# Expert steps of 1024 columns with one PSUM bank pair each for gate and up, in place of 512-column steps on two alternating banks

## What is computed

```python
D_MODEL, SEQ, N_EXPERTS, TOP_K, EXPERT_DIM = 1024, 256, 8, 2, 3584

def swiglu(x, w_gate, w_up, w_down):
    return (jax.nn.silu(x @ w_gate) * (x @ w_up)) @ w_down

def moe_swiglu(x, w_router, b_router, w_gate, w_up, w_down):
    xt = x.reshape(-1, D)
    logits = (xt @ w_router).astype(jnp.float32) + b_router.astype(jnp.float32)
    top_val, top_idx = lax.top_k(logits, TOP_K)
    gates = jax.nn.softmax(top_val, axis=-1)
    combine = jnp.sum(jax.nn.one_hot(top_idx, N_EXPERTS) * gates[..., None], axis=1)
    for e in range(N_EXPERTS):
        out = out + combine[:, e:e + 1] * swiglu(xt, w_gate[e], w_up[e], w_down[e])
    return out
# f(x) of every sub-layer goes into x <- LayerNorm(alpha * x + f(x))
```

## Time and profile before

| | us |
|---|---|
| median of 3 runs (1743.3 to 1747.3) | 1747.09 |
| the profiled execution | 1747.38 |
| its span, first to last instruction | 1745.6 |
| gather of the first link to gather of the second | 123.55 |

### The profile page before, as it was taken

How to read it: one execution, slowest core, us unless ns; L and a number is a source line. 1 busy time by engine, 2 the same in 40 slices (tenths; PEclk the granted TensorE clock), 3 DMA queues, 4 the chain that set the end, 5 groups by cost and what they waited for, 6 DMA issues and landing times.

```text
span 1745.6 us, 22452 instructions
## 1 busy us (share of the span) xinstructions
PE 1617.3 (93%) x8768; PEld 1380.7 (79%) x8768; DVE 1296.6 (74%) x1080; ACT 965.9 (55%) x819; POOL 24.2 (1%) x17
## 2 busy tenths in 40 slices
PE   3978889999799878799999999999999999999995
PEld 3868659998799757688888887888888888888884
DVE  2757455545667565688898898888898988988995
ACT  2332234443243533277777776776776767777772
POOL 1000000000200000000000000000000000000000
PEclk7988989999899998799999999999999999999997
DMA  8160045554454001799999999999999999999990
GB/s 272 49 217 1 1 154 184 192 183 154 144 169 169 25 25 43 271 353 371 346 362 369 341 356 359 340 365 361 351 360 337 362 369 342 364 363 346 369 341 26
DMA packets 214835, 441.04 MB, mean 253 GB/s; under 512 B 11292, under 2 KB 61780, under 8 KB 214740
## 3 DMA queue, kind: packets, MB, share of 16 engines
q1 hardware_dynamic: 208496, 433.96, 69.5%
q10 hardware_dynamic: 6244, 5.73, 1.1%
HBM read 438.61 MB, written 1.05 MB: 252 GB/s over the span
## 4 chain that ended last, share of the span: by engine, by line
PE 87%; DVE 8%; ACT 3%; ACTq 1%; issue 1%; POOL 0%; POOLq 0%; DVEq 0%
PE ps L1987 18%; PE ps L1989 18%; PE ps L1988 17%; PE ps L1547 5%; PE ps L1548 5%; PE ps L1549 5%; PE ps L1540 2%; PE ps L1982 1%; PE ps L2012 1%; DVE w_lo L981 1%; PE ps L1806 1%; PE ps L1807 1%; PE ps L1808 1%; ACTq L586 1%; PE ps L1944 1%
## 5 line engine op out<-in xcount | busy, mean ns | idle before, releaser
L1355 DVE TENSOR_TENSOR w_lo<-raw,w_hi 128x2048 fp32r<-128x2048 f32 x252 | 577.2, 2291 | 90.5 <-ACT w_hi L837 86.3
L837 ACT CAST w_hi<-raw 128x2048 fp32r<-128x2048 f32 x252 | 482.7, 1916 | 174.4 <-PE ps L1989 160.0
L1987 PE MATMUL ps<-w_hi,xg_hi 128*128 128x512 f32 x672 | 268.5, 400 | 5.7 <-DVE xg_lo L1412 3.1
L981 DVE TENSOR_TENSOR w_lo<-raw,w_hi 128x2048 fp32r<-128x2048 f32 (+1 forms) x73 | 168.3, 2312 | 132.0 <-ACT w_hi L632 131.9
L1989 PE MATMUL ps<-w_hi,xg_lo 128*128 128x512 f32 x672 | 262.9, 391 | 0.0
L1988 PE MATMUL ps<-w_lo,xg_hi 128*128 128x512 f32 x672 | 262.2, 390 | 0.0
L1547 PE MATMUL ps<-xT_hi,w_hi 128*128 128x256 f32 x768 | 221.1, 288 | 26.8 <-DVE w_lo L981 21.6
L1548 PE MATMUL ps<-xT_lo,w_hi 128*128 128x256 f32 x768 | 220.3, 287 | 0.0
L1549 PE MATMUL ps<-xT_hi,w_lo 128*128 128x256 f32 x768 | 220.0, 286 | 0.0
L632 ACT CAST w_hi<-raw 128x2048 fp32r<-128x2048 f32 (+1 forms) x73 | 136.3, 1877 | 145.8 <-PE ps L1549 99.1
L1355 DVE TENSOR_TENSOR xT_lo<-raw,xT_hi 128x2048 fp32r<-128x2048 f32 x84 | 192.3, 2289 | 31.6 <-ACT xT_hi L837 31.1
(11 more groups left out here) (346 smaller groups left out, 2244.4 us busy)
## 6 DMA issues: line engine op xcount, KB each, us to landing
raw<-in_moe_w_gate SPq DMA_DIRECT2D x112, 1024.0 KB, 6.5
raw<-in_moe_w_up SPq DMA_DIRECT2D x112, 1024.0 KB, 6.8
raw<-in_moe_w_down SPq DMA_DIRECT2D x112, 1024.0 KB, 6.4
raw<-in_ssm_w_in SPq DMA_DIRECT2D x20, 1024.0 KB, 5.3
raw<-in_ffn_w_gate SPq DMA_DIRECT2D x11, 1024.0 KB, 5.4
raw<-in_ffn_w_up SPq DMA_DIRECT2D x11, 1024.0 KB, 5.5
raw<-in_ffn_w_down SPq DMA_DIRECT2D x11, 1024.0 KB, 4.9
raw<-in_even_w_in SPq DMA_DIRECT2D x10, 1024.0 KB, 12.0
```

The lines of the kernel that those rows point to most:

```text
L837: act.copy(e_hi((n + 2 * odd) % CUT_E), raw[:, i, :]).then_inc(sem("hi_made"), 1)
L981: TTO(w_lo[:, c, 0:size], raw[:, i, 0:size], w_hi[:, c, 0:size].bitcast(F32), ALU.subtract).then_inc(d_lo_made, 1)
L1355: TTO(e_lo(c), raw[:, n % RAW, :], e_hi(c).bitcast(F32), ALU.subtract).then_inc(lo_made, 1)
L1987: mm(out_ap, hi, whi, start=start, stop=False)
```

## The change

`EW` becomes 1024, so an expert has four steps: three of 1024 columns and one of 512 (`step_width`). A piece still has 128 x 2048 numbers, but a gate or up piece of a wide step is 2 row blocks x 1024 columns, in runs of 4 KB, where it was 4 x 512 in runs of 2 KB. A wide step has four gate, four up and four down pieces (`parts`). An expert still has 42 pieces and every piece still 12 matmuls of 512 columns. Gate takes banks 0 and 1, up 2 and 3, in every step; the alternation (`side`) is gone. Gate of step j waits for the silu of step j-1 (`e_silu`), up for its product (`e_h`). `silu` and `mult` are one instruction of 1024 columns. The transposes of a wide step come in two halves of four (`turn_h(it, j, h)`), at the piece counts that `turn_at` gives, and `between` puts them and the scatters behind any piece. The gather goes to banks 7 and 4, from inside `down`. The link now has 8 + 2 pieces: next expert's gate at 40 to 43, up at 44 to 47, last down at 48 and 49. `START` is 8 and `HEAD_END`, where the loop over experts turns round, 32 (was 28). The rest of the kernel is as it was.

```diff
-EW = 512
-ESTEPS = EF // EW
+EW = 1024
+ESTEPS = -(-EF // EW)
-START = 2 * PPU
-HEAD_STEPS = 4
+HEAD_STEPS = 2
+def parts(j):
+    return step_width(j) // 256
+START = 2 * parts(0)
-SCATTER_AT = [START + 5, START + 9, START + 15, START + 21]
-PLACE_G = START + 29
-PLACE_GATHER = START + 33
+SCATTER_AT = [START + 5, START + 9, START + 13, START + 17]
+PLACE_G = place(HEAD_STEPS, 1) + parts(HEAD_STEPS)
+PLACE_GATHER = place(ESTEPS - 2, 2) + 2
+def turn_at(j, h):
+    if j == ESTEPS - 1:
+        return place(ESTEPS, 1)
+    if j == ESTEPS - 2:
+        return place(ESTEPS - 1, h) + 1
+    return place(j + 1, 0) + (1, parts(j + 1))[h]
...
             def expert_rest(it, odd, following):
...
                     if linked and n == PLACE_GATHER + 1:
-                        gathered_high(following)
+                        gathered_high(following, (7, 4))
                     if linked or n + CUT_E < stretch_end(False):
                         cut_high(n + CUT_E, it, odd)
...
-            def product(it, odd, j, what, n):
+            def between(it, done, j, previous):
+                for h in range(parts(j - 1) // 2):
+                    if j and done == turn_at(j - 1, h):
+                        turn_h(it, j - 1, h)
+                if previous is not None and done in SCATTER_AT:
+                    scatter(previous, SCATTER_AT.index(done), 7, 1)
+            def product(it, odd, j, what, n, previous=None):
                 if what == 0:
-                    pe.wait_ge(sem("e_h"), count(ESTEPS, it, (j - 1 if 0 < j < ESTEPS else j) + FIRST))
+                    pe.wait_ge(sem("e_silu"), count(ESTEPS, it, j + FIRST))
+                else:
+                    pe.wait_ge(sem("e_h"), count(ESTEPS, it, j + FIRST))
...
-                        last = three(ps[:, 2 * side(j) + what, :], xg_hi[:, k, :], xg_lo[:, k, :], whi[:, kk, :], wlo[:, kk, :],
-                                     k == 0, k == KD - 1)
+                        for h in range(step_width(j) // 512):
+                            cs = slice(512 * h, 512 * h + 512)
+                            last = three(ps[:, 2 * what + h, :], xg_hi[:, k, :], xg_lo[:, k, :], whi[:, kk, cs], wlo[:, kk, cs],
+                                         k == 0, k == KD - 1)
                     last.then_inc(piece_used, 1)
+                    between(it, n + m + 1, j, previous)
...
             def down(it, odd, j, n, previous=None, following=None):
...
                     last.then_inc(piece_used, 1)
+                    between(it, n + m + 1, 0, previous)
+                    if following is not None and n + m + 1 == PLACE_GATHER:
+                        pe.wait_ge(sem("ehT_made"), count(EF // 512, it, 2 * j + 2 + FIRST))
+                        pe.wait_ge(sem("G_copied"), count(1, it, 1))
+                        gather(following, (7, 4))
...
             def expert_rest(it, odd, following):
                 for j in range(HEAD_STEPS + 1, ESTEPS):
                     product(it, odd, j, 0, place(j, 0))
-                    turn_h(it, j - 1)
                     product(it, odd, j, 1, place(j, 1))
-                    if following is not None and place(j, 1) + 1 == PLACE_GATHER:
-                        pe.wait_ge(sem("e_h"), count(ESTEPS, it, (ESTEPS - 1) + FIRST))
-                        gather(following)
-                    down(it, odd, j - 1, place(j - 1, 2))
+                    down(it, odd, j - 1, place(j - 1, 2), None, following)
                 if following is not None:
                     pe.wait_ge(sem("xg_lo_made"), count(2, following, 2))
                     product(it, odd, ESTEPS, 0, place(ESTEPS, 0))
```

More of the change, by code:

```diff
@@ L113, in place @@
 def place(step, what, linked=True):
-    return START + PPU * (LINKED if linked else LONE).index((step, what))
+    order = LINKED if linked else LONE
+    return START + sum(parts(j) for j, _ in order[:order.index((step, what))])
 def stretch_end(linked):
-    return START + PPU * len(LINKED if linked else LONE)
-SCATTER_AT = [START + 5, START + 9, START + 15, START + 21]
-PLACE_G = START + 29
-PLACE_GATHER = START + 33
+    return START + sum(parts(j) for j, _ in (LINKED if linked else LONE))
+HEAD_END = place(HEAD_STEPS + 1, 0)
+assert stretch_end(True) == PPE + START and stretch_end(False) == PPE
+SCATTER_AT = [START + 5, START + 9, START + 13, START + 17]
[7 more added lines that the diff above has]
+    return place(j + 1, 0) + (1, parts(j + 1))[h]
 C_ID, C_TRI, C_TRIS = 0, P, 2 * P
@@ L506, in _, with load_block @@
                 sp.sem_inc(lo_made, 1)
[L508 to L515, removed]
+            def load_block(e, it, first, j, what):
+                for m in range(parts(j)):
+                    sp.wait_ge(lo_made, count(PPE, it, (first + m + 1)))
+                    i = (first + m) % RAW
+                    if what < 2:
+                        k = 2048 // step_width(j)
+                        src = (eg, eu)[what][e].rearrange("(k p) n -> p k n", p=P)[:, k * m:k * (m + 1), EW * j:EW * j + step_width(j)]
+                    else:
+                        c = EW // P * j + 2 * m
+                        src = ed[e].rearrange("(k p) n -> p k n", p=P)[:, c:c + 2, :]
+                    sp.dma_start(raw[:, i, :].rearrange("p (k n) -> p k n", k=src.shape[1]), src).then_inc(raw_loaded[i], 16)
@@ L527, in link_loads @@
             def link_loads(e, it, following):
                 for what in range(2):
[L530 to L533, removed]
+                    load_block(following, it, place(ESTEPS, what), 0, what)
+                load_block(e, it, place(ESTEPS - 1, 2), ESTEPS - 1, 2)
@@ L535, in last_loads @@
             def last_loads(e, it):
-                for half in range(PPU):
-                    load_piece(e, it, place(ESTEPS - 1, 2, False) + half, ESTEPS - 1, 2, half)
+                load_block(e, it, place(ESTEPS - 1, 2, False), ESTEPS - 1, 2)
             first_loads(0, (0, 0))
```

184 lines of the change are left out of this document (93 added, 91 removed).

## The result

| | before | after |
|---|---|---|
| median, us | 1747.19 (4 runs) | 1779.05 (4 runs, 1772.61 to 1779.8) |
| profiled execution, us | 1747.38 | 1778.55 |
| its span, us | 1745.6 | 1776.8 |
| gather to gather, where the loop doesn't turn, us | 123.55 to 123.59 | 128.09 to 128.23 |

The ratio is 1.0173, with a 95% interval of 1.0158 to 1.0187: the change makes the kernel 1.7% slower. The forecast was 1777.0 us in a range of 1766 to 1785.

The account below looks back on a forecast made before the run. TensorE was taken as the bound. Link stall 21.7, first expert 0.7 and lower clock 7.5 sum to 29.9 us, which from the profiled 1747.4 us, 0.3 above the median of 1747.1, gives 1777.0 us, range 1766 to 1785.

Parts of the forecast that it names:

- The bound: Expert stage: TensorE's own work sets the pace, busy all of an undisturbed expert's 123 us; DMA at 97 to 98% does not.
- The link: Between experts: gathered casts and subtractions queue behind cast 42, so TensorE waits for `xg_lo`; 3.1 us at seven links, 21.7 us.
- The clock: Behind the link's gap: matmuls run at lower clock, 1.5 us at five of seven links, 7.5 us; bounds 0 and 11.
- The first expert: First transposes, with no down pieces as cover: TensorE waits for the product on DVE, 0.7 us, once.
- the work itself: TensorE's matmuls, transposes, gather and scatters in an expert: same counts and pace as before, 0 us.
- The single pair of banks: Gate and up waiting for the previous step's silu and product: enough pieces lie between, 0 us; if late, under 1.2 us per step.
- turn_G: Last `add` only two pieces ahead of it: holds by 0.3 to 0.4 us, 0 us; if missed, up to 3.5 us.
- Longer runs: Gate and up loads in 4 KB runs: land a few tenths sooner, ahead of a cast waiting for TensorE, 0 us.
- 1: Rival: the link's gap leaves the clock alone, all else holds; 1769.5 us, chance 0.13.
- 2: Rival: no stall at the link, only the first expert's 0.7 us left; 1747.8 us, chance 0.05.
- rival 3: Loads set the expert's pace, so longer runs make the kernel faster; 1721 us, chance 0.03.
- 4: Rival: more stalls, at `turn_G` and at the head's transposes behind `output_high`; 1785 to 1795 us, chance 0.09.

Follow-up runs that it names:

- e5_filled_gap: The changed kernel with 22 unused 256-column matmuls on TensorE at each link, before the wait for `xg_lo`: 1769.95 us, ratio 1.0145.
- e1_slot_earlier: The changed kernel with the gathered casts on ACT and gathered subtractions on DVE one iteration earlier, behind the cut of piece 41: 1747.19 us, ratio 1.0005.
- e2_before_slot_later: The kernel before, with only the gathered casts and subtractions one iteration later on ACT and DVE, behind the cut of piece 42: 1776.12 us, ratio 1.0176.
- e3_gather_earlier: The changed kernel with the gather on TensorE one piece earlier, behind piece 36, ACT and DVE as in the change: 1778.27 us, ratio 1.0179.
- e6_slot_later: The changed kernel with the gathered casts and subtractions another iteration later on ACT and DVE, behind the cut of piece 43: 1803.82 us, ratio 1.0334.
- e4: The changed kernel with only DVE's gathered subtractions one iteration earlier, ACT's gathered casts still behind cast 42: 1756.07 us, ratio 1.006.
- e8_before_unrolled: The kernel before, with the loop over experts written out on all engines and nothing else: 1743.10 us, ratio 0.9986.
- e9_wide_again: Rerun of the changed kernel with gathered work one iteration earlier, step 0's first transposes one piece later and the expert loop written out: 1741.66 us, ratio 0.9979.

## Why the prediction was right

*The bound.* TensorE's own work in all of an expert: as read. The rest of a linked expert in the changed kernel is again 112.70 busy of 112.70 us.

*The link.* The step that carries the forecast, in each part: cast 42 first (forecast 848.28 to 850.19, measured 848.54 to 850.46), the low part of piece 42, then `xg_lo` done at 853.7 (853.98), TensorE on again at 853.8 (854.20). Forecast 3.1 us a link; the stall measures 3.2 by e5_filled_gap against e1_slot_earlier. That the slot does it, and not the gather's place, the wide steps or the banks, is shown from three sides by e1_slot_earlier, e2_before_slot_later and e3_gather_earlier.

*The clock.* The price of one was right, 1.5 forecast and 1.6 measured. The count was a choice, five of seven links. In the profiled execution it is seven of seven, in e2_before_slot_later five and in e3_gather_earlier six. With seven the term is 7 x 1.6 = 11.2 us, at the upper bound of 11 that stood there. So this term was 3.7 us too small for this execution, and the prediction had no row that tells five from seven. Nor is the price of one a constant: it was 1.6 us in most cases, but the seventh link of e2_before_slot_later and three links of e6_slot_later lost nearly 3.

*The first expert.* Forecast a wait of 0.7 us at the first transposes. The changed kernel:

```profile
759.10 0.39 PE L2020 MATMUL ps<-w_hi,xg_lo 128*128 128x512 f32 x1
759.95 0.66 PE L2057 MATMUL ps<-const,eh 128*128 128x128 f32 x4 [0.46 <-DVE eh L1445]
```

It starts 759.95 - 759.10 - 0.23 = 0.6 us late. Beside it, the first expert of this execution starts at lower clock for longer than that of the kernel before: from its first product to the gather it takes 842.20 - 731.85 = 110.35 us, where it took 841.94 - 733.84 = 108.10. The difference of 2.25 us holds 1.6 us that the prediction didn't have. The longer start stands in the profile of e2_before_slot_later too, which has the old first expert, and is missing in that of e3_gather_earlier, which has the new one. The profiles of e1_slot_earlier and of e4 to e8 have it as well, that of e8_before_unrolled with the old first expert, and that of e9_wide_again, with the new one, doesn't. So it comes with the execution and isn't the change's; why it comes is open.

*A gain not foreseen.* The well placed wide kernel's gathers are 123.26 us apart, not 123.55. In the kernel before, the first down piece of a linked expert waits for `oe_lo`, which DVE has only just read out of the sum's banks, at 1001.88 + 0.68 = 1002.56:

```profile
1001.88 0.68 DVE L1425 TENSOR_TENSOR oe_lo<-ps,oe_hi 128x512 fp32r<-128x512 f32 x1
1002.30 0.39 PE L1989 MATMUL ps<-xT_hi,xg_lo 128*128 128x512 f32 x1
1002.69 0.49 PE L1987 MATMUL ps<-w_hi,ehT_hi 128*128 128x512 f32 x1
```

That is 0.39 us in place of 0.23, with no idle time shown, since the matmuls' records overlap; with the restart some 0.25 us. The wide steps put that down piece eight pieces behind `output_high` in place of four, and it is gone. I took "the work itself" as 0, and it is about -2 us over seven links. It was in the timeline, but not in the waits.

*The sum for the profiled executions.* Links 7 x 3.2 = 22.4, clock 7 x 1.6 = 11.2, first expert 2.25, the vanished wait -2.1, the two turns of the loop -0.4 (the gathers around them are 129.72 and 129.31 us apart, 2.7 us over two others, in place of 3.1), and the expert stage starts 2.0 us sooner (first gather of the changed kernel at 722.19 against 724.19), in a part of the program that the change doesn't touch. That is 31.4; the spans differ by 31.2. The stall, 22 of these 31 us, was forecast for the right reason. That the whole came out within 2 us of the forecast 29.9 is in part luck: the clock (3.7), the stall (0.7) and the first expert (1.6) were put too low, and against them stand the vanished wait (2.1), the sooner start (2.0) and the turns (0.4), which the forecast didn't have either.

*What was put at nothing.* The single pair of banks and the wide silu and product: no wait for `e_silu`, and for `e_h` none but the first expert's. `turn_G`: none; the last `add` ends 0.28 to 0.35 us ahead of it in all seven experts, which is the cover that was worked out. Longer runs: landings of gate and up went from 6.5 and 6.8 to 6.3 us, those of down, whose runs stayed the same, from 6.4 to 6.6, and the casts' wait is for TensorE as before. The rule on packet overhead (the Trainium skill, "DMA: Bandwidth & Descriptors", section "Why small descriptors are slow (HBM only)") points the same way as the landings of gate and up, but no run here turns it into time, since nothing waits for a landing. The 358 GB/s that the prediction sets as a limit beside its rows isn't one here: in the 40 slices on the page of the kernel before, the expert stage has slices at 369 and 371 GB/s.

*Rivals.* 1, no loss of clock: refuted at the links, and made real only with the gap filled, at 1769.95 us where 1769.5 was given for it. That these two agree to half a microsecond is chance, since the first expert, the vanished wait and the turns moved too. 2 and 3 fell with the result, and e1_slot_earlier shows that rival 3 isn't hidden beneath the stall either. 4: no further stall was there, by the list of TensorE's waits.

## What to carry to other kernels

In a hand-ordered queue it isn't the cover on the consumer's side that counts, but what stands in line ahead of the work: two casts whose data lay ready 2.7 us before cast 42 was released stood behind it, and more lead for their data changed nothing. When steps are resized, check for each moved operation, engine by engine, what the instruction in front of it waits for. And when an engine at full load gets a gap of 3 us, price the gap and then the slower matmuls behind it.

## What the hardware showed unexpectedly

Matmuls whose result nobody uses, put into a gap that is there anyway, gave back 1.6 us a link.

Whether a gap costs the clock is not fixed by its length alone. Seven gaps of 1.14 to 1.25 us never did. Gaps of 2.86 to 3.08 us did at five, six and seven of seven links, in executions of otherwise like links, and gaps of 5.57 to 5.69 us at all seven. Of single gaps in between, 2.69 us (in the dense SwiGLU of the kernel before) and 2.42 us (at a turn in e1_slot_earlier) did, while 1.83, 2.12 and 2.27 us didn't. Nor does the clock always fall with the first matmul behind the gap: after the change it fell some six matmuls later at three of seven links.

And the turn of the loop over experts has a gap of 0.7 to 2.4 us on TensorE, which goes when the loop is written out and which no line of the page names as such.
